# Three output projections and three small products, from fp32 to terms of halves and features

## The reference, cut to what matters

```python
# layer 3 (A_gate, LRU and three-branch attention)
(a_gate, a_x, q, kc, vc, ks, vs, kw, vw, gts) = _split_2(h @ w_in, IN0_SIZES)   # gts: 24 columns
y_a = rg_lru(causal_conv(a_x, conv_w, conv_b), wa, ba, wx, bx, lam) * gelu(a_gate)
y_b = nsa_mixer(q, kc, vc, ks, vs, kw, vw, sigmoid(gts), pe_k, w1_k, w2_k, pe_v, w1_v, w2_v)
x = x + g_m * (concatenate([y_a, y_b]) @ w_out)                                 # l0_out
# inside nsa_mixer: blocks of 32 positions, a learned bias pe added to each, then a small MLP
flat = (kv[idx] + pe).reshape(nc, CMP_LEN * D);  kc = gelu(flat @ w1) @ w2
# layer 4 (index scores choose keys)
q, k, v, q_idx, k_idx, w_idx = _split_2(h @ w_in, IN1_SIZES)                    # w_idx: 8 columns
x = x + g_m * (dsa_mixer(q, k, v, q_idx, k_idx, w_idx) @ w_out)                 # l1_out
```

## Time and profile before

| | |
|---|---|
| median of 3 runs | 2441.29 us (2440.44 to 2444.14) |
| the profiled execution | 2442.06 us, span 2440.2 us |
| PE busy | 2324.9 us (95%), mean granted clock 0.976 |
| DVE, ACT, POOL busy | 1300.9 (53%), 790.2 (32%), 330.4 us (14%) |
| chain of waits, share of PE | 86%, DVE 7%, all others 5% |
| read from HBM | 221.83 MB, 92 GB/s over the span |

### The profile page before, as it was taken

The page is one execution under the profiler, slowest core; times in us unless marked ns, Lnnn a source line. Parts: engine busy times, 40 slices in busy tenths (PEclk is TensorE's granted clock), DMA queues, the critical chain, the costliest instruction groups (busy, mean ns, idle before and its releaser), DMA issues.

```text
span 2440.2 us, 30656 instructions
## 1 busy us (share of the span) xinstructions
PE 2324.9 (95%) x11954; PEld 1765.3 (72%) x11954; DVE 1300.9 (53%) x2864; ACT 790.2 (32%) x1671; POOL 330.4 (14%) x327
## 2 busy tenths in 40 slices
PE   7999999989999999999998999999989999999998
PEld 5866576578546576778775878887877668888876
DVE  3565665652346546455847266666446854433333
ACT  4254103421013106432447132223333462222233
POOL 2200100000000102020100010003432102000154
PEclk9999999999999999999879999999999999999999
DMA  7200331001233552022410045554312101323222
GB/s 298 75 13 35 111 112 46 18 27 37 83 133 98 129 180 51 10 86 88 149 36 1 24 165 191 175 194 165 122 62 75 64 1 69 121 87 104 88 102 78
DMA packets 58269, 225.91 MB, mean 93 GB/s; under 512 B 20478, under 2 KB 21118, under 8 KB 41740
## 3 DMA queue, kind: packets, MB, share of 16 engines
q1 hardware_dynamic: 58124, 223.94, 27.3%
HBM read 221.83 MB, written 2.10 MB: 92 GB/s over the span
## 4 chain that ended last, share of the span: by engine, by line
PE 86%; DVE 7%; POOL 2%; issue 2%; ACT 2%; DMA 1%; SPq 1%; POOLq 0%; DVEq 0%; ACTq 0%
PE PS L86 81%; PE PS L91 5%; POOL WKr L103 1%; DVE WK L108 1%; DVE WK L142 1%; DMA GB<-in_ev_ada 1%; ACT WK L98 1%; SPq L162 1%; DVE WK L103 0%; DVE RINGr L103 0%; DVE WK L130 0%; ACT WK L96 0%; POOL SM L103 0%; DVE ACC L115 0%; DVE WK L115 0%
## 5 line engine op out<-in xcount | busy, mean ns | idle before, releaser
L86 PE MATMUL PS<-Hr,GBr 128*128 128x512 f32 x1284 | 440.7, 395 | 3.5 <-ACT Hr L96 2.2
L86 PE MATMUL PS<-Hr,RINGr 128*128 128x512 f32 x1040 | 405.0, 389 | 0.0
L96 ACT ACTIVATE WK<-PS 128x512 f32<-128x512 f32 (+2 forms) x390 | 189.5, 518 | 519.8 <-PE PS L86 299.9
L86 PE MATMUL PS<-H,RING 128*128 128x512 f32 (+1 forms) x928 | 336.1, 514 | 0.0
L115 DVE SCALAR_TENSOR_TENSOR ACC<-ADA,SM,ACC 128x256 f32<-128x256 f32 x608 | 296.5, 511 | 53.8 <-DMA ADA<-in_l_mod 33.7
L86 PEld LDWEIGHTS PS<-Hr,GBr 128*128 128x128 f32 x1284 | 242.5, 190 | 59.6 <-issue 4.4
L86 PEld LDWEIGHTS PS<-H,RING 128*128 128x128 f32 x928 | 172.1, 190 | 135.5 <-issue 127.6
L103 DVE TENSOR_TENSOR RINGr<-RING,GBr 128x1024 fp32r<-128x1024 f32 x152 | 187.8, 1274 | 138.7 <-ACT GBr L96 138.6
L86 PE MATMUL PS<-RING,GB 128*128 128x256 f32 x1156 | 253.7, 381 | 3.4 <-DVE GB L115 1.2
L86 PEld LDWEIGHTS PS<-RING,GB 128*128 128x128 f32 x1156 | 220.5, 191 | 35.3 <-issue 5.1
L86 PEld LDWEIGHTS PS<-Hr,RINGr 128*128 128x128 f32 x1040 | 198.5, 191 | 40.6
(11 more groups left out here) (215 smaller groups left out, 2894.1 us busy)
## 6 DMA issues: line engine op xcount, KB each, us to landing
ADA<-in_l_mod SPq DMA_DIRECT2D x96, 512.0 KB, 3.8
RING<-in_l_gu SPq DMA_DIRECT2D x44, 1024.0 KB, 4.9
RING<-in_l_wd SPq DMA_DIRECT2D x24, 1024.0 KB, 4.9
RING<-in_ev_in SPq DMA_DIRECT2D x13, 1024.0 KB, 5.8
ADA<-in_od_ada SPq DMA_DIRECT2D x24, 512.0 KB, 3.6
RING<-in_od_in SPq DMA_DIRECT2D x11, 1024.0 KB, 6.5
RING<-in_l_in SPq DMA_DIRECT2D x10, 1024.0 KB, 5.2
RING<-in_l_out SPq DMA_DIRECT2D x8, 1024.0 KB, 4.9
```

The lines of the kernel that those rows point to most:

```text
L86: self.last = self.eng.matmul(out, lhsT, rhs, start=start, stop=stop, skip_group_check=True)
L96: self.last = self.eng.activation(out, in_, func, bias=bias, scale=scale)
```

## The change

1. `od_out`, `l0_out` and `l1_out` become products of halves. PE takes them chunk by chunk (`out_split`): chunk j outside, the four tiles inside, 96 matmuls of 256 columns for each chunk, on all eight banks. DVE adds the four first halves, then the four second halves, each followed by its `each(t)`. The features y are split too: the take-outs of S and D write the rounded y on ACT and its remainder on DVE; in N and the LRU half of S the rounding is ACT's (`y_split`) and the remainder POOL's, for two groups of N DVE's. Chunks 0 and 1 are rounded inside the attention (`OUT_AT`), 2 and 3 and the first chunk of the next stage in `out_rounds`.
2. In projections S the bias pe is first multiplied and summed on DVE (128x2048 and a reduction to 128) and then needs one matmul; gts are made as 24 features of 512 positions (24 matmuls) and turned by four small ones; v0 moves into attention S, one tile in each of iterations 0, 2, 4, 6. The `ada` steps leave this stage; twelve of the operations for each of four tiles stand in the output projection of layer 1 instead, and the later ones move up. `l0_in3` is cut into `l0_in3` and `l0_in4`, and the ring's order follows.
3. The 8 columns of w_idx in layer 4 are made as 8 features of 384 positions: 24 matmuls and three that turn, for 72 of 8 columns.

```diff
-SPLIT = ("l0_in1", "l0_in2", "l0_in3", "l0_gts", "l1_ki", "l1_qi", "l1_kv", "l1_q1", "l0_gu", "l0_wd", "l1_gu", "l1_wd")
+SPLIT = ("od_out", "l0_out", "l1_out", "l0_in1", "l0_in2", "l0_in3", "l0_gts", "l0_in4", "l1_ki", "l1_qi", "l1_kv", "l1_q1", "l0_gu", "l0_wd", "l1_gu", "l1_wd")
...
-                         ("l0_cw1", 2, 2048), ("l0_cw2", 1, 160), ("l0_in2", 1, 2048), ("l0_lru", 1, 1024),
-                         ("l0_in3", 3, 2048),
-                         ("l0_gts", 1, 192), ("l0_out", 4, 2048), ("l0_gu", 22, 2048), ("l0_wd", 12, 2048),
+                         ("l0_cw1a", 1, 2048), ("l0_in2", 1, 2048), ("l0_cw1b", 1, 2048), ("l0_cw2", 1, 160),
+                         ("l0_in3", 1, 2048), ("l0_lru", 1, 1024), ("l0_gts", 1, 192), ("l0_in4", 2, 2048),
+                         ("l0_out", 4, 2048), ("l0_gu", 22, 2048), ("l0_wd", 12, 2048),
...
+        V0_AT = {2 * t: (t,) for t in range(4)}
+        V0_BY = {4 + 3 * t: (t,) for t in range(4)}
...
+        Y_AT = {"N": {11: (0,), 12: (1,), 13: (2,), 14: (3,), 15: (4,), 16: (5,), 17: (6,), 19: (7,)},
+                "S": {10: (0,), 13: (1,), 16: (2,), 19: (3,)}}
...
+        OUT_AT = {"N": {10: "od_out", 18: "od_out+"}, "S": {42: "l0_out", 49: "l0_out+"},
+                  "D": {26: "l1_out", 33: "l1_out+"}}
...
+            def out_split(name):
+
+                for j in range(4):
+                    i, jj, cols = FIRST[name] + j, j // 2, slice(j % 2 * 256, j % 2 * 256 + 256)
+                    Wh, Wl = split_weights(i, 8)
+                    for t in range(4):
+                        if j % 2 == 0:
+                            next_bank(("out", name, t, jj), [(dve_value, ("gated", name, t, jj))])
+                        b, c = where["out", name, t, jj], slice(t * 128, t * 128 + 128)
+                        for k in range(8):
+                            y_ready(name, k)
+                            pe.wait_ge(rest_signal(i), ("rest", i, k // 4))
+                            pe.matmul(bank(b)[:, cols], y_hi(name, k, c), Wh(k, slice(0, 256)), k == 0 and j % 2 == 0,
+                                      False)
+                            pe.matmul(bank(b)[:, cols], y_hi(name, k, c), Wl(k, slice(0, 256)), False, False)
+                            pe.matmul(bank(b)[:, cols], y_lo(name, k, c), Wh(k, slice(0, 256)), False, k == 7)
+                        if j % 2 == 1:
+                            pe.then_inc(pe_product, ("out", name, t, jj))
+                    if j % 2 == 0:
+                        pe.then_inc(pe_product)
+                    chunk_done(i)
...
-                for l in range(16):
-                    pe.matmul(bank(b1, 0, 62), W[:, l, :], kv[:, :, 2 * l:2 * l + 481:16], l == 0, l == 15)
-                    pe.matmul(bank(b2, 0, 1), W[:, l, :], W2[:, 128 + j * 16 + l:129 + j * 16 + l], l == 0, l == 15)
+                b = next_bank(("p", "q0", j, 0), copied("q0", j, 0))
+                for k in range(8):
+                    for l in (2 * k, 2 * k + 1):
+                        pe.matmul(bank(b1, 0, 62), W[:, l, :], kv[:, :, 2 * l:2 * l + 481:16], l == 0, l == 15)
+                    pe.wait_ge(rest_signal(iq), ("rest", iq, k // 4))
+                    pe.matmul(bank(b), Qh(k, c), Hh("l0m", k), k == 0, False)
+                    pe.matmul(bank(b), Qh(k, c), Hl("l0m", k), False, False)
+                    pe.matmul(bank(b), Ql(k, c), Hh("l0m", k), False, k == 7)
+                pe.then_inc(pe_product, ("p", "q0", j, 0))
+                pe.wait_ge(dve_value, ("pe weights", j))
+                pe.matmul(bank(b2, 0, 1), pe_weights(j), ones[:, 0:1], True, True)
                 pe.then_inc(pe_product, ("hid", j))
                 chunk_done(i)
-                ada(4)
-                ada(4)
-            i = FIRST["l0_in2"]
-            for m in range(2):
-                fm_split("l0m", i, m, "q0", m, lambda s0: copied("q0", m, s0))
-                ada(4)
...
+            def branch_gates():
+                i = FIRST["l0_gts"]
+                Wh, Wl = split_weights(i, 8)
+                c, b = slice(0, 24), next_bank(("p", "gts", 0, 0), [(act_value, "gts")])
+                for k in range(8):
+                    pe.wait_ge(rest_signal(i), ("rest", i, k // 4))
+                    pe.matmul(bank(b)[0:24, :], Wh(k, c), Hh("l0m", k), k == 0, False)
+                    pe.matmul(bank(b)[0:24, :], Wh(k, c), Hl("l0m", k), False, False)
+                    pe.matmul(bank(b)[0:24, :], Wl(k, c), Hh("l0m", k), False, k == 7)
+                pe.then_inc(pe_product, ("p", "gts", 0, 0))
+                chunk_done(i)
...
-            tm_split("l0m", i + 2, 0, 256, "v0", lambda t: copied("v0", t, 0))
-            chunk_done(i + 2)
-            i = FIRST["l0_gts"]
-            tm_split("l0m", i, 0, 24, "gts", lambda t: [(act_value, ("gts", t))])
+            branch_gates()
...
+                    tm_split("l0m", FIRST["l0_in4"] + 1, 0, 256, "v0", lambda t: copied("v0", t, 0), (t,))
...
-            def weights_i(t):
-                tm_split("l1m", FIRST["l1_ki"], 128, 8, "wi", lambda t: [(dve_value, ("wi", t))], (t,))
+            def weights_i():
+                i, c = FIRST["l1_ki"], slice(128, 136)
+                (Wh, Wl), b = split_weights(i, 8), next_bank(("p", "wi", 0, 0), [(dve_value, "wi rows")])
+                for k in range(8):
+                    wait_h("l1m", k, 0)
+                    hh, hl = Hh("l1m", k, 128, 512), Hl("l1m", k, 128, 512)
+                    pe.matmul(bank(b, 0, 384)[0:8, :], Wh(k, c), hh, k == 0, False)
+                    pe.matmul(bank(b, 0, 384)[0:8, :], Wh(k, c), hl, False, False)
+                    pe.matmul(bank(b, 0, 384)[0:8, :], Wl(k, c), hh, False, k == 7)
...
+            def out_rounds(name, st, nxt):
+
+                round_chunk(FIRST[name] + 2)
+                for t in range(4):
+                    norm_half(st, t, 0, name)
+                round_chunk(FIRST[name] + 3)
+                round_chunk(FIRST[nxt])
 
...
+                    if tag in OUT_AT and out_chunk(tag, i) is not None:
+                        if tag == "N":
+                            act.wait_ge(dve_max, ("masked", "N", 7, 1))
+                        round_chunk(out_chunk(tag, i))
...
-                if t % 2 == 0:
-                    act.wait_ge(pe_attended, ("attended", tag, u))
-                    act.activation(Gt(t, s0, s1), bank(U["ob"]), ACT.Copy).then_inc(act_value, ("o", tag, u))
+                act.wait_ge(pe_attended, ("attended", tag, u))
+                act.activation(y_hi("l1_out" if tag == "D" else "l0_out", t, ALL), bank(U["ob"]), ACT.Copy)
+                act.then_inc(act_value, ("oh", tag, u))
...
+                    if tag in OUT_AT and out_chunk(tag, i) is not None:
+                        rest(out_chunk(tag, i))
...
-                    dve.tensor_copy(g, o)
+                    name = "l1_out" if tag == "D" else "l0_out"
+                    dve.wait_ge(act_value, ("oh", tag, u))
+                    if tag == "S":
+                        dve.wait_ge(pe_product, ("chunk", FIRST["l0_in4"] + 1))
+                    dve.tensor_tensor(y_lo(name, t, ALL), o, y_hi(name, t, ALL), ALU.subtract)
...
+            def out_split(name, st, each, nxt):
+
+                rest(FIRST[name] + 2)
+                for t in range(4):
+                    add(name, st, t, 0, where["out", name, t, 0], "c2" if st != "od" else "c", t)
+                rest(FIRST[name] + 3)
+                rest(FIRST[nxt])
+                for t in range(4):
+                    add(name, st, t, 1, where["out", name, t, 1], "c2" if st != "od" else "c", t)
                     each(t)
                 dve_value.at["gates done", st] = dve_value.n
 
...
             for t in range(5):
                 norm_half("od", t, 0, "ev_out")
                 norm_half("od", t, 1, "ev_out")
+                if t < 4:
+                    ada(3)
...
+                each = WK[:, 0:2048].rearrange("p (l o) -> p l o", l=16)
+                by = W2[:, 128 + j * 16:144 + j * 16].rearrange("p (l o) -> p l o", o=1).broadcast_to([128, 16, 128])
+                dve.wait_ge(ring_in[i2 % NRING], ("ring", i2))
+                dve.wait_ge(ring_in[i % NRING], ("ring", i))
+                own(dve.tensor_tensor(each, ring_view(i, 16), by, ALU.mult).then_inc(dve_value))
+                dve.tensor_reduce(pe_weights(j), each.rearrange("p l o -> p o l"), AXX, ALU.add)
+                dve.then_inc(dve_value, ("pe weights", j))
...
+                copy_out("q0", j, 0, 512)
+                if j == 0:
+                    rest(FIRST["l0_in3"])
...
-            i = FIRST["l0_in3"]
-            rest(i)
+            copy_out("q0", 2, 0, 512)
             lru_tile(0)
-            rest(i + 1)
-            for m in range(2):
-                copy_out("q0", 2 + m, 0, 512)
-                lru_tile(1 + m)
-            rest(i + 2)
-            for m in range(2):
-                copy_out("ks", m, 0, 512)
-                if m == 0:
```

(51 more changed lines are left out.)

280 lines of the change are left out of this document (179 added, 101 removed).

## The result

The changed kernel took 2463.43 us (median of 4, 2458.24 to 2473.51), the kernel before 2440.86 (median of 4): a ratio of 1.0078, interval 1.0047 to 1.0110. It is slower, and outside the range of 2414 to 2454. The profiled execution took 2464.14 us, span 2462.3; PE is busy 2286.6 us of it, 38 less than before, and the time grew by 22: PE is idle 176 us instead of 115.

A forecast was written before the change was run, and what follows sets the result against it. The prediction took PE's chain of waits as the bound, and DVE in projections S's LRU stretch. Its terms summed to -5.1 us: 2442.06 to 2437.0 profiled, 2436.2 in the median's terms, range 2414 to 2454.

The forecast's parts named there:

- What bounds, and the outputs' terms: PE's chain of waits bounds, DVE in projections S's LRU stretch; output od +4.7 us, l0 and l1 -6.1 each.
- Four ends in series: Outputs: DVE finishes four tiles one after another, 7.5 us each in od, 4.04 in l0 and l1.
- Half clock at six places, +3.5: Outputs' starts and ends: after waits PE runs at half clock, losing 0 to 2.2 us each; +3.5 (0 to 13).
- Attention N and its end, +4.0: Attention N: roundings and remainders inside +1 us (0 to 4.4), at its end +3.0 (0 to 5).
- Projections S, -22.5: Projections S: 103.3 us become 80.8, with PE idle some 12 ahead of ks0; -22.5 (-27 to -15).
- Attention D, +10.4: Attention D: take-outs in series on ACT and DVE, a chunk's rounding and remainders, the end; +10.4 us (2 to 14).
- The term in series: Attention D: two-step take-out delays the next unit's maxima by 0.78 us, seven banks, 5.4 (0 to 5.4).
- Index weights, -3.4: w_idx products: 8.2 us at full clock become 4.8 with 24 wide matmuls and the turn; -3.4.
- Attention S, +10.4: Attention S: v0 net +3.5 us, take-outs 2.3, y roundings 0.6, chunk 0 2.7, end 1.3; +10.4 (0 to 16).
- The term of -8: Attention S: v0 keeps PE denser, so the first 26.1 us at clock 0.64 run in some 19; -8 us.
- Rival 2: Attention S begins and stays at half clock: no relief (+8), v0 slower (+9), +12 in all, 2453 us; chance 0.20.
- Its condition: Attention S: the half-clock rival decides once v0's first two tiles are issued at the lower level, 0.21 us a product.

The follow-up runs named there:

- e3: Changed kernel with the tiles' ends of the three outputs overlapped (second half of tile t+1 added before tile t is scaled): 2447.38 us, ratio to before 1.0016.
- e4: Changed kernel with DVE's half of the take-out in attentions S and D one iteration later: 2450.38 us, ratio to before 1.0025.
- e7: e1 with the four y roundings of attention S in iterations 0 to 3 instead of 10 to 19: 2451.85 us in one execution.
- e9: Changed kernel with outputs, take-outs and their surroundings as before and v0 in projections S, leaving the small products: 2422.85 us, ratio to before 0.9912.
- e10: e9 with v0 in attention S as in the change, nothing else added there: 2428.01 us in one execution.
- e11: e9 with ks0's and gts' remainders on DVE and their roundings on ACT ahead of lru_tile(1): 2416.57 us, ratio to before 0.9879.
- e2: Changed kernel without the y split in mid attention S (ACT's roundings, POOL's remainders; result not the kernel's): 2460.90 us, ratio to before 1.0072.
- e1: Changed kernel with all 96 products of v0 back at the end of projections S: 2464.37 us, ratio to before 1.0082.
- e6: Changed kernel with chunks 0 and 1 of l0_out and l1_out rounded in the last two iterations of attentions S and D: 2461.73 us in one execution.
- e8: Changed kernel with e3, e4 and e7 together, plus the outputs' last two chunks taken tile by tile: 2443.03 us, ratio to before 0.9982.

## Why the prediction was wrong, point by point

The forecast was -5.1 and the two profiles are 22.1 apart, 27 more: attention S 17 of it, projections S 7, the early stretch that no edit touches 5; the others cancel to within 2.

- **What bounds, and the outputs' terms: right.** Four ends in series were forecast at 7.5 and 4.04 us; they measured 7.5 and 4.03. Output od took 70.6 (67.8 forecast), l0 and l1 fell by 4.2 and 4.3 (6.1 forecast). e3 shows the mechanism.
- **Half clock at six places, +3.5: too small.** What the slow first 11 us of the three outputs lose (granted clock 0.78 in od, 0.84 in l0 and in l1) is 2.5, 1.7 and 1.7 us, nearly all of what they took over the forecast: 2.8, 1.9 and 1.9. Output od with the norm behind it, forecast +4.7, measured +7.8.
- **Attention N and its end, +4.0: right.** At equal clock in the early stretch output od begins at 1013.4 and 1014.0 (e4, e7) with the split and at 1009.0 and 1009.2 (e9, e10) without, +4.6.
- **Projections S, -22.5: too much, -15.1** (from PE's first hidden product, as the forecast counted), at the very edge of its own range of -27 to -15. PE's 11.8 us in front of ks0 are there as forecast (12), but they begin later: ks0 starts 62.1 us into the stage and not 55.9. The reductions of the bias took 3.69 and 3.58, not 2.3, and PE waited 6.5 us for them; DVE's wait ahead of `lru_tile(0)` was 8.5, not 4.5. e11 shows that the wait ahead of ks0 was the bound.
- **Attention D, +10.4: measured +13.1**, and +17 in the executions at the lower clock. The term in series was 0.74 a period for 0.78 (e4).
- **Index weights, -3.4**: projections D fell by 8.2, of which 5.4 is that the same stretch of before stood at lower clock (0.95 against 0.99); some 3 remain. The feed-forward ahead of it fell by 4.2 at 1.00 against 0.98; nothing in the sum stands for that.
- **Attention S, +10.4: the step that failed; measured +27.3.** It said that "a PE kept denser by v0" gives back 8 of v0's 11.5 us (26.1 down to 19 would be 7.1 by its own figures). The first half of that came true, the clock of the first 26.1 us rose from 0.64 to 0.83; the second didn't. e10 alone puts v0 there: +11.3, next to nothing back. And e11 shows what the higher clock is worth there without v0: 0.87 for 0.67, and the stage 1.5 us shorter (its later part stood at 0.98 for 1.00, which hides at most 1.6 more). The term of -8 isn't there in any run.
- **The other parts of attention S:** y roundings taken as 0.6 in all, 5.8 (e2); the take-outs' series 3.4 (e4, 2.3 forecast); the rest, 27.3 - 11.3 - 5.8 - 3.4 = 6.8, are the two chunks' rounding, the end and the clock (4.0 forecast), not told apart further; with e1's 8.7 for v0, taken from the changed kernel itself, the rest is 9.4. e6 only shows that the chunks' place hardly matters.
- **Rival 2 (slower by the half clock)** came nearest in sign and not in mechanism. Its condition nearly held: v0's first block and most of the second ran at 0.21 us a product. But from 1259.3 on v0's products follow at 0.12: attention S didn't stay at the lower level, it lost its clock later. Behind the first 26.1 us the granted clock is 0.89 in the changed kernel and 0.98 in e10, where y's roundings, the split take-outs and the chunks are missing; in the whole stage it is 0.88 against 0.91 before, which makes 6.5 us of the 27.3 (0.12 x 134.4 less 0.09 x 107.1). The chunk shown at e6 is one such place: a wait of 3.1 us, then 0.50.
- **The price left out**: executions of the same stretch before output od differ. Of the 22 us between the two profiles some 5 are that. How much of it is left between medians of four isn't known.
- **The count of products was right and beside the point.** Three outputs of 45.9 instead of 55.5 us do save 28.8 us of PE. Mended (e8), they pay it all for rounding weights, remainders and splitting y beside the attentions. How much more than all is less sure: e9 without them is 20 us faster than e8 by the medians (ratios to before 0.9912 and 0.9982), but by the stages of the two profiles only 6, and the other 15 lie ahead of output od, where e8's early stretch stood at 0.92 and e9's at 0.98.

The Trainium skill ("TensorE: Matmul & The Clock Gate", section "Wait — 56ns, not 53.3ns?") states a floor of about 25 ns between the starts of two matmuls. Taken as their price, it would have made the features for gts a loss of 3 us, by the prediction's estimate. The trace shows that it isn't the price here: the 96 narrow products took 15.9 us at clock 0.66, the 24 wide ones follow at 0.23, 5.5 us. Going by the trace was right.

## What to carry to other kernels

Find out what a slow clock costs before counting on its relief: here a stage with 0.87 for 0.67 in its first 26 us was only 1.5 us shorter. Work put into an engine's in-order queue fills its waits only if the wait's cause doesn't stand behind that work: in a pipeline of scores, maxima and turned products a block of foreign products delays the cause by its own length. Before shortening one engine's products by splitting operands, add up what the splitting asks of the other engines in the stages next to it; here it was at least as much as was saved. When a loop over chunks is put outside the loop over tiles, all tiles' ends come together, so their steps have to be interleaved (add t+1, then scale t), or they stand in series; and an operation that waits for another engine belongs behind the work that is ready.
